# A transformer trunk's first step: the order of its roundings, products, turns and loads is changed

## The reference

```
def rms_norm(x, g):
    y = x * rsqrt(mean(x * x, -1) + EPS)
    return y * g

def swiglu_half_step(h, norm_g, w_gate_up, w_down):
    hn = rms_norm(h, norm_g)
    gate, up = split(hn @ w_gate_up, 2, axis=-1)
    return h + 0.5 * ((silu(gate) * up) @ w_down)

# reference(...): h = x; per layer: swiglu_half_step, mixer with attention to mem,
# swiglu_half_step
```

## Time and profile before

| | before |
|---|---|
| median of 3 runs | 937.53 us (937.19 to 938.5) |
| the profiled execution | 937.63 us |
| its span, first to last instruction | 935.8 us |
| TensorE busy | 929.6 us (99%) |
| DVE busy | 556.3 us (59%) |
| ScalarE busy | 461.8 us (49%) |
| HBM traffic | 178 GB/s over the span |

### The profile page before, as it was taken

One profiled execution on the slowest core, in us unless ns is written; L12 is line 12 of the kernel. 1 busy time (PEld: TensorE's weight loads), 2 busy tenths in 40 slices (PEclk: granted clock), 3 DMA queues, 4 the chain that ended last, 5 costly groups with the idle time before them and its releaser, 6 DMA issues.

```text
span 935.8 us, 13327 instructions
## 1 busy us (share of the span) xinstructions
PE 929.6 (99%) x4448; PEld 763.1 (82%) x4448; DVE 556.3 (59%) x701; ACT 461.8 (49%) x652; POOL 49.9 (5%) x82
## 2 busy tenths in 40 slices
PE   9999999999999999999999999999999999999998
PEld 6888888887888888888878888888888788888887
DVE  6655464585666555464687545555777765464553
ACT  6654444465545444453554435444666554443441
POOL 2010110003000000000000000000221000000000
PEclk9999999999999999999999999999999999999999
DMA  8787566455147646556366665656433276566441
GB/s 293 257 265 215 174 192 212 160 162 173 46 123 246 216 155 202 182 181 222 91 183 207 217 201 169 204 166 202 137 116 118 65 244 204 175 189 215 156 158 45
DMA packets 136863, 166.98 MB, mean 178 GB/s; under 512 B 10776, under 2 KB 101632, under 8 KB 136832
## 3 DMA queue, kind: packets, MB, share of 16 engines
q1 hardware_dynamic: 135472, 164.67, 55.6%
q0 software_dynamic: 1184, 1.83, 0.8%
q10 hardware_dynamic: 176, 0.07, 0.0%
HBM read 165.48 MB, written 1.05 MB: 178 GB/s over the span
## 4 chain that ended last, share of the span: by engine, by line
PE 95%; DVE 1%; ACT 1%; issue 1%; DMA 1%; SPq 1%; DVEq 0%; ACTq 0%
PE ps L1519 22%; PE ps L1521 21%; PE ps L1520 21%; PE ps L1587 8%; PE ps L1589 8%; PE ps L1591 8%; PE ps L1571 2%; PE ps L1454 1%; PE ps L1727 1%; DMA h<-in_x_dram 1%; PE ps L1758 1%; PE ps L1714 1%; PE ps L1747 0%; DVE w_lo L984 0%; DVE z L1013 0%
## 5 line engine op out<-in xcount | busy, mean ns | idle before, releaser
L984 DVE TENSOR_TENSOR w_lo<-w_raw,w_hi 128x1024 fp32r<-128x1024 f32 x296 | 356.8, 1224 | 147.5 <-ACT w_hi L652 144.9
L652 ACT CAST w_hi<-w_raw 128x1024 fp32r<-128x1024 f32 x296 | 304.3, 1051 | 133.5 <-PE ps L1591 73.1
L1519 PE MATMUL ps<-w_hi,mainT_hi 128*128 128x512 f32 x768 | 306.0, 398 | 0.9 <-DVE mainT_lo L1022 0.3
L1521 PE MATMUL ps<-w_hi,mainT_lo 128*128 128x512 f32 x768 | 299.8, 390 | 0.0
L1520 PE MATMUL ps<-w_lo,mainT_hi 128*128 128x512 f32 x768 | 299.2, 390 | 0.0
L1519 PEld LDWEIGHTS ps<-w_hi,mainT_hi 128*128 128x128 f32 x768 | 144.2, 188 | 33.0 <-DVE w_lo L984 2.1
L1521 PEld LDWEIGHTS ps<-w_hi,mainT_lo 128*128 128x128 f32 x768 | 144.2, 188 | 31.0
L1520 PEld LDWEIGHTS ps<-w_lo,mainT_hi 128*128 128x128 f32 x768 | 144.5, 188 | 28.0
L705 ACT ACTIVATE silu_g<-ps,row_rs 128x256 f32<-128x256 f32 x88 | 41.8, 476 | 230.0 <-PE ps L1521 230.0
L1069 DVE SCALAR_TENSOR_TENSOR act_f<-ps,row_rs,silu_g 128x256 f32<-128x256 f32 x88 | 42.6, 484 | 159.7 <-ACT silu_g L705 159.7
L1587 PE MATMUL ps<-w_hi,actT_hi 128*128 128x512 f32 x320 | 99.1, 391 | 0.0
(11 more groups left out here) (193 smaller groups left out, 661.9 us busy)
## 6 DMA issues: line engine op xcount, KB each, us to landing
w_raw<-in_ffn_w_gate_up_dram SPq DMA_DIRECT2D x352, 256.0 KB, 3.6
w_raw<-in_ffn_w_down_dram SPq DMA_DIRECT2D x176, 256.0 KB, 4.1
w_raw<-in_w_in_dram SPq DMA_DIRECT2D x32, 256.0 KB, 3.3
w_raw<-in_w_out_dram SPq DMA_DIRECT2D x32, 256.0 KB, 3.4
w_raw<-in_w_mem_kv_dram SPq DMA_DIRECT2D x16, 256.0 KB, 3.4
w_raw<-in_w_kv_dram SPq DMA_DIRECT2D x8, 256.0 KB, 3.3
ycat<-in_mem_dram SPq DMA_DIRECT2D x1, 1024.0 KB, 7.2
out_dram<-h SPq DMA_DIRECT2D x4, 256.0 KB, 2.0
```

The source lines that it names most:

```text
L652: ins = nc.scalar.copy(half(w_hi[s], b), half(w_raw[s], b))
L984: ins = nc.vector.tensor_tensor(half(w_lo[s], b), half(w_raw[s], b), half(w_hi[s], b).bitcast(F32), ALU.subtract)
L1519: pe.matmul(dst, x_hi, wh, start=start, stop=False)
L1521: return pe.matmul(dst, x_lo, wh, start=False, stop=stop)
```

## The change

- Two of the first seven products on zeros are left out.
- ScalarE casts x's first quarter of tile 0 ahead of the weight's first chunk; DVE makes their low parts in the same order.
- ScalarE's row sum of tile 0 moves ahead of the split of the second half and of `high_first(4)`; DVE's `low_first(4)` moves behind the split of the second half and the scaling of tile 1's.
- Within a first piece the order becomes x_hi w_hi, x_lo w_hi, x_hi w_lo. The first two wait for the high weight only, the third for the low weight.
- Piece (0, 1) goes ahead of the two turns of the second quarter, piece (2, 0) ahead of the turn of tile 0's second half, (3, 0) ahead of that of tile 1, and (3, 1) ahead of (4, 0).
- SyncE issues both units of the second step's gate and up weights ahead of the down weight, both of whose halves come behind.

```diff
-WARM_PRODUCTS = (7, 3)
+WARM_PRODUCTS = (5, 3)
...
                     load_gate_up(name, 1, (0,) if name == "ffn0" else (0, 1))
-                    load_down(name, 0, halves=(0,) if name == "ffn0" else (0, 1))
                     if name == "ffn0":
                         load_gate_up(name, 1, (1,))
-                        load_down(name, 0, halves=(1,))
+                    load_down(name, 0)
+                    if name == "ffn0":
                         sp.dma_start(ycat[:, :, :], a["mem"][0].rearrange("(t p) d -> p t d", p=P)).then_inc(mem_landed, 16)
...
+            split_first(0)
             high_first(0)
-            split_first(0)
             split_gained(0)
...
             high_first(3)
+            row_sum("H0", 0)
+            split("H0", 0, 1)
             high_first(4)
-            split("H0", 0, 1)
-            row_sum("H0", 0)
             high_first(5)
...
             scale_first(0)
+            split_first(0)
             low_first(0)
-            split_first(0)
             split_gained(0)
...
             scale("H0", 0, 1)
-            low_first(4)
             split("H0", 0, 1)
             scale("H0", 1, 1)
+            low_first(4)
             low_first(5)
...
                 if t == 0:
                     if k % 2:
+                        pe.wait_ge(hi_ready[s], kk // 2 + 1)
+                    else:
+                        pe.wait_ge(first_hi, k // 2 + 1)
+                dst = ps[:, GU_BANK + t, :]
+                x_hi, x_lo = (x[:, k, t * P:(t + 1) * P] for x in (tr_hi["main"], tr_lo["main"]))
+                pe.matmul(dst, x_hi, w_hi[s][:, kk, :], start=k == 0, stop=False)
+                pe.matmul(dst, x_lo, w_hi[s][:, kk, :], start=False, stop=False)
+                if t == 0:
+                    if k % 2:
                         pe.wait_ge(lo_ready[s], kk // 2 + 1)
                     else:
                         pe.wait_ge(first_lo, k // 2 + 1)
-                mm = three(ps[:, GU_BANK + t, :], tr_hi["main"][:, k, t * P:(t + 1) * P], tr_lo["main"][:, k, t * P:(t + 1) * P],
-                           w_hi[s][:, kk, :], w_lo[s][:, kk, :], k == 0, k == KC - 1)
+                mm = pe.matmul(dst, x_hi, w_lo[s][:, kk, :], start=False, stop=k == KC - 1)
...
             def first_step():
                 first_piece(0, 0)
+                first_piece(0, 1)
                 turn_first(0, 1)
                 turn_first(1, 1)
-                first_piece(0, 1)
                 first_piece(1, 0)
                 first_piece(1, 1)
+                first_piece(2, 0)
                 turn_h("H0", 0, 1)
-                first_piece(2, 0)
                 first_piece(2, 1)
+                first_piece(3, 0)
                 turn_h("H0", 1, 1)
-                first_piece(3, 0)
-                for k in range(4, KC):
+                first_piece(3, 1)
+                first_piece(4, 0)
+                for k in range(5, KC):
                     first_piece(k, 0)
                     first_piece(k - 1, 1)
                 first_piece(KC - 1, 1)
```

## The result

| | before | after |
|---|---|---|
| median | 937.62 us (937.12 to 938.82, 8 runs) | 940.00 us (939.35 to 942.33, 8 runs) |
| ratio | | 1.0029, 95% interval 1.002 to 1.0038 |
| profiled execution, its span | 937.63, 935.8 us | 940.69, 938.9 us |
| TensorE busy | 929.6 us | 929.4 us |

The change costs 2.4 us by the two medians (0.25%), 2.7 us by the ratio (0.29%). The forecast was 938.6 us, 936.8 to 939.7: the direction was right, the time lies outside the range, and the case that it came out by, the transfers (rival 3), had been given a chance of 0.04.

The account below looks back on a forecast made before the run. TensorE, busy 99% of the span, was taken to bound the kernel, transfers at most in the first 36 us. First step 1.0 us later, transfer order hidden: 937.6 + 1.0 = 938.6 us, range 936.8 to 939.7.

Parts of the forecast that it names:

- rival 3: Transfers: a hole over 1.3 us delays the memory input past TensorE; 939.6 us for a hole of 2.3; chance 0.04.
- Down weight behind: SyncE's queue, waiting for low weights 5 and 7: holes of nothing and 0.2 us in the transfers, hidden.
- the margin: Memory input lands at 26.4 to 26.6, TensorE turns it at 27.6; a hole costs only from 1.3 us on.
- 6 us of backlog: DMA queue: transfers already issued, landing 6.1 us after issue, keep the engines busy; the evidence against the transfers' case.
- The first step: Start of the kernel up to piece (4, 1): starts at 17.0 instead of 16.11, 1.0 us later with its second start.
- dearest edit: Piece (2, 0) ahead of the turn of x's second half: turn goes from 10.41 to 11.85, 1.4 us late.
- DVE's order: Low weight 4 moved behind leaves DVE idle from 13.15 to 13.85; the remaining operations follow in line, done 16.95.
- The clock: TensorE's start: fewer warming products delay the clock's rise, twelve products at 0.43 us, 0.9 on top, 939.5; chance 0.12.

Follow-up runs that it names:

- e2: The changed kernel with the old transfer order, everything else of the change kept; 938.66 us, ratio 1.0011.
- e4: The changed kernel with the old transfer order and the old order of pieces and turns on TensorE; 937.84 us, ratio 1.0002.
- e6: The changed kernel with the old transfer order and only the two quarter turns back ahead of piece (0, 1); 937.87 us, ratio 1.0004.
- e7: The changed kernel with the old transfer order and only the turn of tile 0's second half back ahead of piece (2, 0); 938.24 us, ratio 1.0005.
- e8: e4 with DVE's low weight 4 moved back ahead of the split of the second half; 938.86 us, ratio 1.0012.
- e10: The kernel before without any warming product, nothing else changed; 938.63 us, ratio 1.001.
- e1: The kernel before with only the down weight moved behind both gate units; 941.6 us, ratio 1.0036.
- e3: The changed kernel with the memory input issued between unit 0 and unit 1 of the gate weights; 938.56 us, ratio 1.0008.
- e5: The changed kernel with the memory input issued behind both gate units and ahead of the down weight; 938.47 us, ratio 1.0009.
- e9: The kernel before with five warming products instead of seven, nothing else changed; 937.89 us, ratio 1.0002.

## Why the prediction was wrong

**The step that failed** is the one under "Down weight behind": "What was issued keeps the engines busy to about 17.75 ... so the first hole is nothing and the second 0.2 us". It took the landing of a transfer for the end of its data. The DMA view of the kernel after, over 16 to 18 us, in slices of 0.05 us:

```profile
DMA  9887865544421111100239623979599957998999
GB/s 287 266 266 246 246 205 184 184 164 164 144 82 62 41 61 41 61 21 0 82 102 164 143 102 102 246 225 205 184 287 348 266 205 266 348 389 307 369 348 328
```

The last transfer issued ahead of the wait (at 12.1) lands at 17.4, but the flow thins from 16.0 on and is zero at 16.9. The next one was issued at 16.0 and its data starts at 17.0, 1.0 us later (the prediction took 1.2; the rows that it names, 0.74 to 1.7, give 1.0 too). So the landing comes 0.5 us behind the last data. For the flow not to thin, an issue would have been needed at about 15.0, 2.4 us ahead of the last landing (an estimate from these rows). The landing that the prediction took was besides that of the kernel before, 6.1 us behind its issue; the same transfers of the kernel after land 4.9 and 5.3 behind theirs. The Trainium skill, page "DMA: Bandwidth & Descriptors", section "Anatomy of one DMA — SWDGE (gpsimd) path", says that most of a transfer's fixed time is completion after the last byte. It describes another issuing path. These rows agree that there is such a time, but they do not show it as the larger part: 0.5 us behind the last data, 1.0 us ahead of the first.

In windows of 2 us the kernel after has 194 and 241 GB/s over 16 to 18 and 18 to 20 us, before 369 and 353. The two holes are so (369 - 194) x 2 = 350 KB and (353 - 241) x 2 = 224 KB, or 0.9 and 0.6 us at 370 GB/s, in place of nothing and 0.2 us.

A second thing was missed: the rate doesn't come back at once. With much work issued again (four down transfers and the memory input between 18.7 and 21) it was 292 GB/s from 20 to 24 us, against 380 before: another 350 KB, 1.0 us. With the holes that makes the 2.5 us, and the memory input comes 3.3 us late, 1.6 of it by its later issue.

A third term was too large, the margin. The prediction let a hole cost only from 1.3 us on, with the input landing at 26.4 to 26.6 for a turn at 27.6. e2 has the late step without the new order, and there the input lands at 27.35 for a turn at 27.50: the late step, by its late low weights, had used up all but 0.15 us of the margin. From there the new order adds 2.15 us to the landing (29.5) and the stop of 2.25 us.

Rival 3 had the mechanism, and that each further microsecond costs one; its chance was too low because its evidence "against", 6 us of backlog, was read off landings.

**The first step.** 1.0 us forecast; 1.1 measured in e2, within the bounds 0.7 to 1.4. The mechanism (turns late behind pieces that wait) is shown by e4. Which turn is dearest was likely wrong: "This is the dearest edit", said of the half's turn, belongs to the quarter turns by the medians of e6 and e7. A reason that fits e6's profile: with the quarters back (2, 0) starts at 10.02 without a wait, so the half's turn behind it, at 10.73, is late by 0.3 only.

**DVE's order.** Its idle time was forecast (0.7 us, from 13.15 to 13.85; measured 0.69, up to 13.44), the conclusion that the moved low weight 4 is at fault was not tested there, and e8 refutes the plain form of it.

**The clock.** Not the cause of the loss in the profiled execution: from 6.24 on no product there goes at 0.43 us, and the granted clock from 26 to 38 us is 1.00. Its price was about right: twelve slow products were put at 0.9 us, e10 with ten shows 1.0. One of the eight executions after, 942.33 us, has a mean granted clock of 0.998, like e1's four; it may hold a drop like e1's, but it was not profiled.

**The sum.** e2 and after differ by 1.3 us in their medians; with the first step's 1.1 that is the 2.4. The profiled execution after (940.69) is one of the longer ones, and shows the wait at 2.25. In the median execution the wait would have to be some 1.3 us; no trace shows that.

No version beat the kernel before. e3 and e5 take away the wait, e4 and e6 the late turns; e4 and e6 are equal to it within their intervals, e3 and e5 stay 1.0 and 0.8 us above it in the median.

## What to carry to other kernels

Before a load is moved behind others, look at what its queue does there: a load that needs no free buffer is the filler while the queue waits for buffers, and moving it turns that wait into a hole for everything behind. Read the end of a backlog from the flow of bytes, never from landing times, and then ask which transfer of those behind is wanted first. In a list written by hand, a turn or a copy that starts a long chain goes ahead of a product that may wait, and two engines' lists are only changed together.

## What the runs showed of the hardware

A wait of 2.55 us on TensorE was followed, about 1 us after the work began again, by a stretch of halved clock (products at 0.43 us, granted 0.57 over 30 to 34 us), which cost 1.6 us on top; the wait of 2.2 us in the profile after was not (granted 1.00 over the same window).

The end of the slow stretch at the start isn't fixed (its products start 0.43 us apart, the pace of the 1.2 GHz level, though the granted clock of e9's windows from 6 to 10 us reads 1.00): the same five warming products in front gave products of full speed from 5 us in the profile after and from 10.4 in e9. e9's eleven times lie between 937.28 and 938.87, its slow-started one at 938.64; that the clock makes this spread was seen in that one profile, and not shown for the others.

A load of 256 KB issued by SyncE at 16.0 into a nearly empty queue had its first data 1.0 us later and landed 2.7 us after the issue; an earlier one landed 0.5 us after the flow had reached zero.

After the holes the rate was at most 320 GB/s, in slices of 0.5 us, from 18.5 until 23.5 us on the timeline, though transfers were queued from 19 on. With the memory input's 4 KB packets in place of the down weight's 2 KB ones (e5) it was no faster than e1, 310 GB/s over 20 to 24 us. The engines were not mostly idle: their busy share over 20 to 24 us was 0.95 against 1.05 before, while the rate was 292 against 380. Why is open; no run here tells a shallow queue from an uneven load of the sixteen engines.
